# Turning the normalised tiles of one layer for the Strassen products: sums before the turning, or behind it

## The chip, the cores and the metric

One NeuronCore of a Trainium2 chip runs the whole layer as one program. The metric is device time in microseconds (us), the median of the runs shown. Engines are TensorE (PE in the profile; its weight loads are PEld), VectorE (DVE), ScalarE (ACT), GpSimd (POOL) and SyncE (SP, which issues the DMAs).

## The reference, cut to what matters

```python
h = h + jnp.concatenate([oA, oB], axis=-1) @ w_out     # output projection, 1024 tokens x 1024
hn = rms_norm(h, norm_ffn)
ab = hn @ w_ffn_in                                     # 1024 x (2 * 2816)
h = h + (gelu(causal_conv(ab[:, :2816]) + conv_b) * ab[:, 2816:]) @ w_ffn_out
```

Everything is float32. What is at stake is the stretch from the output projection to the first products of `hn @ w_ffn_in`.

## The kernel before, in words

Every float32 operand of a matmul is split in a high and a low part of type `fp32r`: ACT copies (that rounds, "hi"), VectorE subtracts the copy from the original ("lo"), and three matmuls take the place of one (hi hi, hi lo, lo hi). Each engine has its own program, written out in order by hand, with waits on semaphores; the order in which an engine's work stands is the order in which it runs.

**The projection.** `h` is 8 tiles of 128 tokens. They are projected in the order `O_TILE = (0, 4, 1, 5, 2, 6, 3, 7)`; below, tile i is the i-th of that order, and a pair j is tiles 2j and 2j+1, that is, a tile of the first 512 tokens and its partner in the second 512. Six rows of weights (`O_ROWS`) are left for this loop: `oproj(i, rows)` issues 6 matmuls of 128x512 for each row, so 36 for a tile, into PSUM banks 0 and 1 (even i) or 2 and 3 (odd i). Tiles 0 and 1 are begun earlier; the loop on TensorE runs over i = 2 to 7. For each tile VectorE adds the result to `h` (L1469, signals `h_mid`), ACT squares it (L796), VectorE makes the mean (L1194), GpSimd raises it to -0.5 (L687), and VectorE writes the normalised tile to `xs[:, i % 2]` (L1474, signals `xs1_ready`). SyncE stores each `h` tile to DRAM (L574), so that its place can take the token sums `hx`.

**The Strassen operands.** `hn @ w_ffn_in` is done by Winograd's form of Strassen's algorithm with 7 products. In it the token side needs, with B11, B21 (first tokens, first and second 512 features) and B12, B22 (second tokens), all with features on the partitions: B11, B21, B22 and the sums T1 = B12 - B11, T2 = B22 - T1, T3 = B22 - B12, T4 = B21 - T2. Features are put on the partitions by a transpose on TensorE: a matmul with the identity, 128x128 at a time. Before, the sums are made from the normalised tiles in SBUF: T1, T2, T4 on VectorE (L1410 through `minus`, in the loop behind the odd tile), T3 on GpSimd (L714), into the buffers `t_tmp`. Then TensorE turns them: `x_turn(g, j)` with g = 1: the even tile (8 transposes, L1729), g = 2: T1 and B22 (4 + 4), g = 3: T2 and T3 (4 + 4), g = 4: T4 (4; all of these L1968). The numbers `turn_no` give the order of the 16 groups, `turn_bank` alternates banks 4 and 5 with 6 and 7. Each group is split from PSUM, the high part by ACT's `x_hi(g, j)` (L793), the low part by VectorE's `x_lo(g, j)` (L1185). In the loop on odd i the groups of the pair before stand between rows of weights; the last pair's groups 2, 3 and 4 stand among the first products.

**The first products.** The 22 blocks f of 128 columns of `w_ffn_in` (a block holds one of the conv half and one of the gate half) give 7 products each: `p1` to `p7`, 12 matmuls of 128x512, each into a bank of its own (`bank_of`). `order` lists them: p1 and p2 of blocks 0 and 1, then p6, p7, p5, p4, p3 of block 0, of block 1, and then 7 of each further block. Their weight operands are split into a ring of 9 places by `op_hi(k)` and `op_lo(k)`; k is the position in `order`, so operands 0 to 3 are those of p1 and p2. Weight sums: s1 and s3 on GpSimd (L717, L714), s2 and s4 on VectorE (L1410). `p1_out` (ACT) copies product 1 out of its bank, and `c11(f)` (VectorE, L1499) adds product 2 to it; `p2(f)` for f >= 1 waits for `c11` of the block before, as they share bank 1. "Product 6" below is p6 of block 0.

```python
        def p2(f):
            if f >= 1:
                pe.wait_ge(S.c11, f)
            product(2, f, x_b21)
```

Of the kernel before, what the change touches and what calls it, by code (L numbers as in the profile page):

```python
# [63 lines left out]
def build(nc, x, p, w_in, w_out, sinks, lambda_q, lambda_k, subln_gain, rel_bias, norm_mix, norm_ffn,  # L64
# [140 lines left out]
    t_tmp = {1: conv[:, 0:HALF], 2: conv[:, HALF:D], 3: u3_buf, 4: a_buf[:, HALF + 4:D + 4]}  # L205
# [43 lines left out]
    def u_raw(s):  # L249
# [3 lines left out]
    turn_no = {(1, 0): 1, (2, 0): 2, (3, 0): 3, (1, 1): 4, (4, 0): 5, (2, 1): 6, (3, 1): 7, (1, 2): 8, (4, 1): 9,  # L253
               (2, 2): 10, (3, 2): 11, (1, 3): 12, (4, 2): 13, (2, 3): 14, (3, 3): 15, (4, 3): 16}

    def turn_bank(g, j):
        return 4 if turn_no[g, j] % 2 else 6
# [16 lines left out]
    t_tok t3_tok op_hi op_lo prod s1 s2 s3 s4 p1_out u2 u4 tap0 c11 c12 c21 c22 conv_done gelu_done  # L274
# [403 lines left out]
    def _(pool):  # L678
# [40 lines left out]
        def s1(f):  # L719
            w_there(pool, f, 1)  # L720
            if f == 0:
                pool.wait_ge(S.oproj, 1)
            if f == 1:
                pool.wait_ge(S.tr1, turn_no[2, 3])
                pool.wait_ge(S.t_tok, 4)
            if f >= 2:
                pool.wait_ge(S.op_lo, nth[5, f - 1] + 1)
            plus(s_tmp(1, f), w_half(f, 1, 0), w_half(f, 1, 1), S.s1)

        def s3(f):  # L730
            w_there(pool, f, 0)
            if f == 0:
                pool.wait_ge(S.tr1, turn_no[2, 3])
                pool.wait_ge(S.t_tok, 4)
                pool.wait_ge(S.t3_tok, 4)
            else:
                pool.wait_ge(S.op_lo, nth[7, f - 1] + 1)
            minus(s_tmp(3, f), w_half(f, 0, 0), w_half(f, 1, 0), S.s3)

        for i in range(NT):  # L740
            power(stat[:, i:i + 1], stat[:, 8 + i:9 + i], S.ms1, S.pow1, i)
            if i % 2 == 1:
                pool.wait_ge(S.xs1_ready, i + 1)
                if i >= 3:
                    pool.wait_ge(S.tr1, turn_no[3, i // 2 - 1])
                minus(t_tmp[3], xs[:, 1, HALF:D], xs[:, 1, 0:HALF], S.t3_tok)
            if i == 4:
                s1(0)
# [42 lines left out]
    def _(act):  # L791
# [221 lines left out]
        def x_hi(g, j):  # L1013
            act.wait_ge(S.tr1, turn_no[g, j])
            b = turn_bank(g, j)
            src = ps[:, b:b + 2, :]
            if g <= 2:
                t = j + 4 * (g - 1)
                copy(act_t[:, 0, :, t * P:(t + 1) * P], src.rearrange("p b (k n) -> p (b k) n", k=4), S.xhi1)
            elif g == 3:  # L1020
                act.wait_ge(x_again[j], 32)
                act.wait_ge(x_again[j + 4], 32)
                copy(hx[:, :, 0:HALF].rearrange("p (u j) n -> p u j n", u=2)[:, :, j, :], src, S.xhi1)
            else:
                copy(t4x[:, j, 0:HALF], ps[:, b, :], S.xhi1)

        for i in range(NT):
            j = i // 2
            if i == 2:
                x_hi(1, 0)  # L1030
            if i >= 3 and i % 2 == 1:
                x_hi(2, j - 1)
                x_hi(3, j - 1)
                if i == NT - 1:
                    op_hi(2)
                    op_hi(3)
                x_hi(1, j)
                x_hi(4, j - 1)
            act.wait_ge(S.h_mid, i + 1)
            if i >= 2:  # L1040
                act.wait_ge(S.tr1, turn_no[1 + i % 2, j - 1])
                act.wait_ge(S.t_tok, j)
                act.wait_ge(S.t3_tok, j)
# [29 lines left out]
        op_hi(4)  # L1073
        x_hi(2, 3)
        x_hi(3, 3)
# [99 lines left out]
    def _(dve):  # L1175
# [241 lines left out]
        def s4(f):  # L1417
            if f == 0:
                dve.wait_ge(S.tr1, turn_no[2, 3])
                dve.wait_ge(S.t3_tok, 4)  # L1420
            dve.wait_ge(S.s2, f + 1)
            minus(s_tmp(4, f), w_half(f, 0, 1), s_tmp(2, f)).then_inc(S.s4, 1)
# [18 lines left out]
        def x_lo(g, j):  # L1441
            dve.wait_ge(S.xhi1, turn_no[g, j])
            b = turn_bank(g, j)
            src = ps[:, b:b + 2, :]
            if g <= 2:
                sl = slice((j + 4 * (g - 1)) * P, (j + 4 * (g - 1) + 1) * P)
                low(act_t[:, 1, :, sl], src.rearrange("p b (k n) -> p (b k) n", k=4), act_t[:, 0, :, sl], S.xlo1)
            elif g == 3:
                dst = hx[:, :, :].rearrange("p (u j) n -> p u j n", u=2)[:, :, j, :]
                low(dst[:, :, HALF:D], src, dst[:, :, 0:HALF], S.xlo1)  # L1450
            else:
                low(t4x[:, j, HALF:D], ps[:, b, :], t4x[:, j, 0:HALF], S.xlo1)
# [3 lines left out]
        for i in range(NT):  # L1456
            t, j, b = O_TILE[i], i // 2, 2 * (i % 2)
            if i == 2:
                x_lo(1, 0)
            if i >= 3 and i % 2 == 1:  # L1460
                x_lo(2, j - 1)
                x_lo(3, j - 1)
                if i == NT - 1:
                    op_lo(2)
                    op_lo(3)
                x_lo(1, j)
                x_lo(4, j - 1)
# [253 lines left out]
    def _(pe):  # L1721
# [244 lines left out]
        def turn4(src, bank):  # L1966
            for k in range(4):
                ins = nc.tensor.transpose(ps[:, bank, k * P:(k + 1) * P], src[:, k * P:(k + 1) * P], ident[:, :])  # L1968
            return ins

        def x_turn(g, j):
            n, b = turn_no[g, j], turn_bank(g, j)
            if n >= 3:
                pe.wait_ge(S.xlo1, n - 2)
            if g == 1:
                pe.wait_ge(S.xs1_ready, 2 * j + 1)
                turn8(xs[:, 0, :], b, S.tr1)
            elif g == 2:
                pe.wait_ge(S.t_tok, j + 1)
                turn4(t_tmp[1], b)  # L1980
                turn4(xs[:, 1, HALF:D], b + 1).then_inc(S.tr1, 1)
            elif g == 3:
                pe.wait_ge(S.t3_tok, j + 1)
                turn4(t_tmp[2], b)
                turn4(t_tmp[3], b + 1).then_inc(S.tr1, 1)
            else:
                turn4(t_tmp[4], b).then_inc(S.tr1, 1)

        for i in range(2, NT):
# [3 lines left out]
            if i == 2:  # L1993
                oproj(i, O_ROWS[1:3])
                x_turn(1, 0)
                oproj(i, O_ROWS[3:])
            elif i % 2 == 1:
                x_turn(2, j - 1)
                oproj(i, O_ROWS[1:2])
                x_turn(3, j - 1)  # L2000
                oproj(i, O_ROWS[2:4])
                x_turn(1, j)
                oproj(i, O_ROWS[4:5])
                x_turn(4, j - 1)
# [203 lines left out]
```

## Time and profile before

| | us |
|---|---|
| median of 3 runs | 1230.97 |
| lowest and highest run | 1227.92, 1232.18 |
| span of the profiled execution | 1229.7 |
| TensorE busy in it | 1197.1 (97%) |
| VectorE, ScalarE, GpSimd busy | 867.3 (71%), 517.8 (42%), 250.2 (20%) |

The span runs from the first to the last instruction of the profiled execution; of that execution's own time no other figure is given than this span. A busy share is an average over stages. Which wait ends last in a stage is read from the chain of waits and from the timelines, where each line gives start, duration, engine, code line, output and inputs, how many instructions are merged in it, and in brackets how long the engine was idle before it and which instruction ended that. The duration of a merged TensorE line reaches to the modelled end of its last matmul, which overlaps the next line; lengths of stretches on TensorE are therefore taken from start to start.

### The profile page before, as it was taken

Reading aid. Unit: us, or ns where it says so; the run is one execution under the profiler, and the core shown is the slowest. Engines: PE = TensorE matmul, PEld = TensorE weight load, DVE = VectorE, ACT = ScalarE, POOL = GpSimd, SP = SyncE. Lnnn points to the kernel's source line nnn. Section 1 sums busy time; section 2 is a strip of 40 time slices with the busy share of each in tenths; the row PEclk is TensorE's granted clock in tenths of the full one; section 3 lists DMA queues with packets and bytes.
Section 4 is the critical chain, followed back from the end, with each engine's and each line's share of the span. In section 5 each row is a group of like instructions: output and inputs, shape, how many; then the busy total and the mean of one; then the engine's idle time right before and its main releaser. Section 6 shows DMA issues by size and latency. Waiting matters only on the chain.

```text
span 1229.7 us, 17128 instructions
## 1 busy us (share of the span) xinstructions
PE 1197.1 (97%) x6167; PEld 1001.8 (81%) x6167; DVE 867.3 (71%) x1514; ACT 517.8 (42%) x1045; POOL 250.2 (20%) x291
## 2 busy tenths in 40 slices
PE   8999999999888999999999999999999999999997
PEld 7998887788676888888888888888888888888886
DVE  5433786877886577877787777877777999964443
ACT  4312665565655224433343343343344444733321
POOL 0000000344455122232332323323210000000000
PEclk9999999999899999999999999999999999999999
DMA  7464233111831512242322333233499533620101
GB/s 217 89 90 91 50 89 76 42 40 69 222 139 42 164 52 81 82 128 94 121 87 89 125 103 112 95 94 112 146 345 312 172 95 103 225 75 26 43 35 51
DMA packets 127916, 136.08 MB, mean 111 GB/s; under 512 B 15714, under 2 KB 93274, under 8 KB 127770
## 3 DMA queue, kind: packets, MB, share of 16 engines
q1 hardware_dynamic: 127834, 135.00, 36.1%
q8 instruction: 49, 0.80, 0.3%
q14 instruction: 33, 0.27, 0.1%
HBM read 96.77 MB, written 37.22 MB: 109 GB/s over the span
## 4 chain that ended last, share of the span: by engine, by line
PE 61%; issue 4%; DVE 2%; POOL 1%; ACT 1%; POOLq 0%; DVEq 0%; ACTq 0%
PE ps L1723 60%; PE ps L1729 1%; DVE xs L1474 1%; DVE h L1469 0%; DVE conv L1410 0%; POOL stat L687 0%; ACT xs L796 0%; DVE act_t L1185 0%; POOL stat L706 0%; POOL bias_a L712 0%; POOL more_f L714 0%; PE ps L2118 0%; ACT wbuf L793 0%; POOL o_t L709 0%; DVE h L1688 0%
## 5 line engine op out<-in xcount | busy, mean ns | idle before, releaser
L1723 PE MATMUL ps<-act_t,wbuf 128*128 128x512 f32 x1200 | 280.1, 389 | 0.5 <-DVE a_buf L1499 0.5
L1723 PEld LDWEIGHTS ps<-act_t,wbuf 128*128 128x128 f32 x1200 | 225.2, 188 | 47.5 <-DVE a_buf L1499 0.8
L1723 PE MATMUL ps<-wbuf 128*128 128x512 f32 x912 | 214.8, 390 | 0.0
L1723 PEld LDWEIGHTS ps<-wbuf 128*128 128x128 f32 x912 | 170.6, 188 | 35.1
L1723 PE MATMUL ps<-act_t,wq 128*128 128x512 f32 x624 | 152.2, 396 | 3.6 <-DVE wq L1187 3.0
L1723 PEld LDWEIGHTS ps<-act_t,wq 128*128 128x128 f32 x624 | 114.3, 188 | 30.8 <-issue 7.5
L687 POOL TENSOR_TENSOR stat<-stat 128x1 f32<-128x1 f32 x32 | 17.6, 549 | 420.9 <-DVE stat L1194 420.9
L793 ACT ACTIVATE wbuf<-raw 128x512 fp32r<-128x512 f32 (+1 forms) x107 | 69.0, 646 | 73.9 <-PE ps L1723 63.8
L1723 PE MATMUL ps<-hx,wbuf 128*128 128x512 f32 x408 | 95.7, 389 | 0.0
L1185 DVE TENSOR_TENSOR wbuf<-raw,wbuf 128x512 fp32r<-128x512 f32 (+1 forms) x107 | 87.4, 818 | 11.5 <-ACT wbuf L793 11.2
L1723 PEld LDWEIGHTS ps<-hx,wbuf 128*128 128x128 f32 x408 | 76.5, 188 | 15.9
L875 ACT ACTIVATE e_t<-ps,small 128x128 f32<-128x128 f32 (+7 forms) x64 | 47.3, 740 | 63.4 <-DVE small L1314 62.3
L793 ACT ACTIVATE wbuf<-xs 128x512 fp32r<-128x512 f32 x66 | 39.8, 624 | 71.9 <-DVE xs L1410 54.2
L1723 PE MATMUL ps<-wbuf,act_t 128*128 128x512 f32 x288 | 69.6, 395 | 0.0
L1723 PEld LDWEIGHTS ps<-wbuf,act_t 128*128 128x128 f32 x288 | 52.9, 188 | 10.5
L1723 PE MATMUL ps<-wq,act_t 128*128 128x384 f32 (+1 forms) x384 | 59.5, 315 | 1.5 <-DVE wq L1185 1.5
L1723 PEld LDWEIGHTS ps<-wq,act_t 128*128 128x128 f32 x384 | 57.9, 193 | 2.0 <-issue 1.7
L1723 PE MATMUL ps<-act_t,more 128*128 128x512 f32 x240 | 56.8, 389 | 0.0
L714 POOL TENSOR_TENSOR wbuf_f<-wbuf_f 128x512 f32<-128x512 f32 x33 | 52.2, 1581 | 18.6 <-DVE wbuf_f L1553 15.6
L1185 DVE TENSOR_TENSOR a_t<-ps,a_t 128x512 fp32r<-128x512 f32 (+4 forms) x64 | 44.6, 715 | 15.4 <-ACT a_t L793 15.3
L1723 PEld LDWEIGHTS ps<-act_t,more 128*128 128x128 f32 x240 | 45.0, 188 | 9.4
L1185 DVE TENSOR_TENSOR wbuf<-xs,wbuf 128x512 fp32r<-128x512 f32 x66 | 50.3, 762 | 0.5
(208 smaller groups left out, 1962.8 us busy)
## 6 DMA issues: line engine op xcount, KB each, us to landing
u_ops<-wbuf_f SPq DMA_DIRECT2D x77, 256.0 KB, 2.2
raw<-u_ops SPq DMA_DIRECT2D x77, 256.0 KB, 2.7
raw<-in_w_ffn_in SPq DMA_DIRECT2D x33, 512.0 KB, 3.8
g_ffn<-in_w_ffn_in SPq DMA_DIRECT2D x11, 512.0 KB, 3.9
act_f<-in_w_ffn_out SPq DMA_DIRECT2D x21, 256.0 KB, 4.3
w_raw<-in_w_in SPq DMA_DIRECT2D x10, 512.0 KB, 4.4
wbuf_f<-in_w_ffn_out SPq DMA_DIRECT2D x18, 256.0 KB, 5.9
x_in<-in_x SPq DMA_DIRECT2D x8, 512.0 KB, 3.8
```

Of the source, the lines that this page charges most:

```text
L687: nc.gpsimd.tensor_tensor(dst, src, stat[:, 63:64], ALU.pow).then_inc(done, 1)
L714: nc.gpsimd.tensor_tensor(dst, a, b, ALU.subtract).then_inc(done, 1)
L793: nc.scalar.activation(dst, src, ACT.Copy, scale=scale).then_inc(done, 1)
L875: nc.scalar.activation(e_t[:, pr, m, 0:w], psf[:, at:at + w], ACT.Exp, scale=-1.0, bias=small[:, o + 2 + m:o + 3 + m], accum_out=small[:, ...
L1185: ins = nc.vector.tensor_tensor(dst, src, hi.bitcast(F32), ALU.subtract)
L1474: nc.vector.scalar_tensor_tensor(out=xs[:, i % 2, :], in0=h[:, t, :], scalar=stat[:, 8 + i:9 + i], in1=g_ffn[:, :], op0=ALU.mult, op1=ALU. ...
L1723: return nc.tensor.matmul(dst, lhs, rhs, start=start, stop=stop)
L1729: ins = nc.tensor.transpose(psf[:, bank * HALF + k * P:bank * HALF + (k + 1) * P], src[:, k * P:(k + 1) * P], ident[:, :])
```

## The change

Only plain tiles are turned, one group of 8 transposes for each tile: `x_turn(1, j)` the even tile into banks 4 and 5 (B11, B21), `x_turn(2, j)` the odd tile into banks 6 and 7 (B12, B22). In the loop over i the turning of tile i-1 stands behind the fourth row of weights; in i = 2 both tiles of pair 0 are turned. The last tile is turned behind p2(0). Then ACT copies B12 to SBUF (`x_b12`), VectorE makes T3 = B22 - B12, T1, T2 and T4 from PSUM and the copy, and the splits of T1 to T4 read SBUF. B22 alone is a fifth split, g = 5. `split_no` numbers the splits. GpSimd's T3 is gone. On VectorE `x_sum3` stands ahead of the even tile's h add, T1, T2, the low split of B22 and T4 (`x_sums`) between that add and the mean, and three low splits behind the normalised tile. Behind the loop the order on VectorE, ACT and TensorE changes too.

```diff
-    t_tmp = {1: conv[:, 0:HALF], 2: conv[:, HALF:D], 3: u3_buf, 4: a_buf[:, HALF + 4:D + 4]}
+    t_tmp = {1: u3_buf, 2: conv[:, 0:HALF], 3: conv[:, HALF:D], 4: a_buf[:, HALF + 4:D + 4]}
...
+    def turn_no(g, j):
+        return 2 * j + g
+
+    def split_no(g, j):
+        order = [(1, 0)] + [o for j in range(4) for o in ((5, j), (3, j), (2, j), (4, j), (1, j + 1)) if o != (1, 4)]
+        return order.index((g, j)) + 1
...
             power(stat[:, i:i + 1], stat[:, 8 + i:9 + i], S.ms1, S.pow1, i)
-            if i % 2 == 1:
-                pool.wait_ge(S.xs1_ready, i + 1)
-                if i >= 3:
-                    pool.wait_ge(S.tr1, turn_no[3, i // 2 - 1])
-                minus(t_tmp[3], xs[:, 1, HALF:D], xs[:, 1, 0:HALF], S.t3_tok)
             if i == 4:
                 s1(0)
...
+        def x_b12(j):
+            act.wait_ge(S.tr1, turn_no(2, j))
+            copy(t_tmp[1], ps[:, 6, :], S.b12_out)
 
         for i in range(NT):
             j = i // 2
             if i == 2:
                 x_hi(1, 0)
+            if i >= 2 and i % 2 == 0:
+                x_b12(j - 1)
+                x_hi(5, j - 1)
+            if i == NT - 1:
+                op_hi(2)
+                op_hi(3)
             if i >= 3 and i % 2 == 1:
-                x_hi(2, j - 1)
-                x_hi(3, j - 1)
-                if i == NT - 1:
-                    op_hi(2)
-                    op_hi(3)
                 x_hi(1, j)
-                x_hi(4, j - 1)
...
             square(h[:, O_TILE[i], :], xs[:, i % 2, :], stat[:, 56 + i % 2:57 + i % 2], S.sq1)
+            if i >= 2 and i % 2 == 0:
+                x_hi(3, j - 1)
+                x_hi(2, j - 1)
+                x_hi(4, j - 1)
...
         p1_out(0)
         op_hi(4)
+        x_b12(3)
+        x_hi(5, 3)
+        x_hi(3, 3)
         x_hi(2, 3)
-        x_hi(3, 3)
         op_hi(5)
         x_hi(4, 3)
         op_hi(6)
...
+        b11, b21, b22 = ps[:, 4, :], ps[:, 5, :], ps[:, 7, :]
+
+        def x_sum3(j):
+            dve.wait_ge(S.b12_out, j + 1)
+            dve.wait_ge(S.xhi1, split_no(5, j))
+            minus(t_tmp[3], b22, t_tmp[1]).then_inc(S.t3_made, 1)
+
+        def x_sums(j):
+            dve.wait_ge(S.t3_made, j + 1)
+            minus(t_tmp[1], t_tmp[1], b11).then_inc(S.t_made, 1)
+            dve.wait_ge(S.t_made, 3 * j + 1)
+            minus(t_tmp[2], b22, t_tmp[1]).then_inc(S.t_made, 1)
+            x_lo(5, j)
+            dve.wait_ge(S.t_made, 3 * j + 2)
+            minus(t_tmp[4], b21, t_tmp[2]).then_inc(S.t_made, 1)
...
             if i == 2:
                 x_lo(1, 0)
+            if i >= 2 and i % 2 == 0:
+                x_sum3(j - 1)
+            if i == NT - 1:
+                op_lo(2)
+                op_lo(3)
             if i >= 3 and i % 2 == 1:
-                x_lo(2, j - 1)
-                x_lo(3, j - 1)
-                if i == NT - 1:
-                    op_lo(2)
-                    op_lo(3)
                 x_lo(1, j)
-                x_lo(4, j - 1)
             dve.wait_ge(S.oproj, i + 1)
             nc.vector.tensor_tensor(h[:, t, :], ps[:, b:b + 2, :].rearrange("p b n -> p (b n)"), h[:, t, :],
                                     ALU.add).then_inc(S.h_mid, 1)
+            if i >= 2 and i % 2 == 0:
+                x_sums(j - 1)
             dve.wait_ge(S.sq1, i + 1)
             mean_eps(stat[:, 56 + i % 2:57 + i % 2], stat[:, i:i + 1], D, S.ms1)
...
-            if i % 2 == 1:
...
-                link(minus(t_tmp[1], xs[:, 1, 0:HALF], xs[:, 0, 0:HALF]))
-                link(minus(t_tmp[2], xs[:, 1, HALF:D], t_tmp[1]))
...
-                minus(t_tmp[4], xs[:, 0, HALF:D], t_tmp[2]).then_inc(S.t_tok, 1)
+            if i >= 2 and i % 2 == 0:
+                x_lo(3, j - 1)
+                x_lo(2, j - 1)
+                x_lo(4, j - 1)
             if i in (4, 6):
                 op_lo(i // 2 - 2)
...
         op_lo(4)
-        c11(0)
+        x_sum3(3)
+        x_sums(3)
+        x_lo(3, 3)
         x_lo(2, 3)
-        x_lo(3, 3)
         op_lo(5)
         x_lo(4, 3)
+        c11(0)
         op_lo(6)
...
         def x_turn(g, j):
+            pe.wait_ge(S.xs1_ready, 2 * j + g)
+            if j >= 1:
+                pe.wait_ge(S.t_made, 3 * j)
+                if g == 1:
+                    pe.wait_ge(S.xlo1, split_no(1, j - 1))
+                else:
+                    pe.wait_ge(S.xlo1, split_no(5, j - 1))
+            turn8(xs[:, g - 1, :], 2 + 2 * g, S.tr1)
...
             if i == 2:
                 oproj(i, O_ROWS[1:3])
                 x_turn(1, 0)
-                oproj(i, O_ROWS[3:])
...
+                oproj(i, O_ROWS[3:5])
+                x_turn(2, 0)
                 oproj(i, O_ROWS[5:])
             else:
-                oproj(i, O_ROWS[1:])
+                oproj(i, O_ROWS[1:4])
+                x_turn(1 + (i + 1) % 2, (i - 1) // 2)
+                oproj(i, O_ROWS[4:])
...
         pe.wait_ge(S.h_mid, NT - 1)
-        pe.wait_ge(S.xlo1, turn_no[1, 3])
+        pe.wait_ge(S.xlo1, split_no(1, 3))
         p1(0)
         p2(0)
+        x_turn(2, 3)
         p1(1)
-        x_turn(2, 3)
-        x_turn(3, 3)
         p2(1)
-        x_turn(4, 3)
         pe.wait_ge(S.h_mid, NT)
-        pe.wait_ge(S.xlo1, turn_no[3, 3])
+        pe.wait_ge(S.xlo1, split_no(3, 3))
         p6(0)
-        pe.wait_ge(S.xlo1, turn_no[4, 3])
         for f in range(2):
             if f == 1:
                 p6(1)
             p7(f)
+            if f == 0:
+                pe.wait_ge(S.xlo1, split_no(2, 3))
             p5(f)
+            if f == 0:
+                pe.wait_ge(S.xlo1, split_no(4, 3))
             p4(f)
             p3(f)
```

## Rows read from the trace of the kernel before

**Rows 1.** The page: busy time of the engines; a group of DMA issues (us to landing last).

```profile
PE 1197.1 (97%) x6167; PEld 1001.8 (81%) x6167; DVE 867.3 (71%) x1514; ACT 517.8 (42%) x1045; POOL 250.2 (20%) x291
...
raw<-in_w_ffn_in SPq DMA_DIRECT2D x33, 512.0 KB, 3.8
```

**Rows 2.** The chain that ended last: start, us, what, up to the gate stage.

```profile
486.64 598.44 PE ps L1723 x2640
```

**Rows 3.** Timeline of TensorE in the projection: start, us, what, idle before.

```profile
416.73 1.03 PE L1729 MATMUL ps<-ident,xs 128*128 128x128 f32 x8
...
442.74 0.60 PE L1968 MATMUL ps<-ident,conv 128*128 128x128 f32 x4
...
448.92 1.09 PE L1729 MATMUL ps<-ident,xs 128*128 128x128 f32 x8
449.77 1.64 PE L1723 MATMUL ps<-wbuf,act_t 128*128 128x512 f32 x6
451.25 0.60 PE L1968 MATMUL ps<-ident,a_buf 128*128 128x128 f32 x4
```

**Rows 4.** The same timeline, first products: product 1, the fourth product, product 6.

```profile
472.57 5.61 PE L1723 MATMUL ps<-act_t,more 128*128 128x512 f32 x24
...
483.17 3.03 PE L1723 MATMUL ps<-act_t,wbuf 128*128 128x512 f32 x12 [0.53 <-DVE a_buf L1499]
...
486.40 3.91 PE L1723 MATMUL ps<-hx,wbuf 128*128 128x512 f32 x16
```

**Rows 5.** Timeline of VectorE: sums, h add, mean, tile; c11 and splits.

```profile
419.17 0.69 DVE L1410 TENSOR_TENSOR conv<-xs 128x512 f32<-128x512 f32 x1
419.90 1.67 DVE L1410 TENSOR_TENSOR conv<-xs,conv 128x512 f32<-128x512 f32 x1
...
441.58 1.23 DVE L1469 TENSOR_TENSOR h<-ps,h 128x1024 f32<-128x1024 f32 x1 [0.47 <-PE ps L1723]
444.02 0.15 DVE L1194 TENSOR_SCALAR stat<-stat 128x1 f32<-128x1 f32 x1 [1.22 <-ACT xs L796]
444.83 2.30 DVE L1474 SCALAR_TENSOR_TENSOR xs<-h,stat,g_ffn 128x1024 f32<-128x1024 f32 x1 [0.66 <-POOL stat L687]
...
476.03 1.29 DVE L1474 SCALAR_TENSOR_TENSOR xs<-h,stat,g_ffn 128x1024 f32<-128x1024 f32 x1 [0.67 <-POOL stat L687]
...
482.44 0.68 DVE L1499 TENSOR_TENSOR a_buf<-ps,wbuf_f 128x512 f32<-128x512 f32 x1
483.04 1.21 DVE L1185 TENSOR_TENSOR act_t<-ps,act_t 128x1024 fp32r<-128x1024 f32 x1
484.17 1.21 DVE L1185 TENSOR_TENSOR hx<-ps,hx 128x1024 fp32r<-128x1024 f32 x1
```

**Rows 6.** Timeline of ACT: high splits from PSUM, of 512 and 1024 columns.

```profile
432.03 0.60 ACT L793 ACTIVATE wbuf<-ps 128x512 fp32r<-128x512 f32 x1 [0.81 <-PE ps L1968]
...
450.05 1.03 ACT L793 ACTIVATE act_t<-ps 128x1024 fp32r<-128x1024 f32 x1 [2.96 <-PE ps L1729]
```

**Rows 7.** Timeline of GpSimd: T3 of pair 0, and s1 of block 0.

```profile
419.22 1.80 POOL L714 TENSOR_TENSOR more_f<-xs 128x512 f32<-128x512 f32 x1 [1.40 <-DVE xs L1474]
...
444.77 1.28 POOL L717 TENSOR_TENSOR gel<-raw 128x512 f32<-128x512 f32 x1
```

**Rows 8.** Windows of TensorE: stretch, its length, busy (instructions), granted clock, DMA share, GB/s.

```profile
26.00:30.00 4.00, 3.96 (x18) 0.57 0.41 131
319.00:327.00 8.00, 5.97 (x32) 0.57 1.03 259
388.00:392.00 4.00, 4.00 (x19) 0.57 0.00 0
402.00:1085.00 683.00, 682.35 (x3065) 1.00 0.40 132
```

**Rows 9.** Timeline of TensorE in the attention stage: two idle times ahead of falls.

```profile
317.78 0.30 PE L1898 MATMUL ps<-ident,bias_a 128*128 128x128 f32 x1 [1.61 <-POOL bias_a L712]
...
387.04 1.06 PE L1915 MATMUL ps<-ident,e_t 128*128 128x128 f32 x8 [2.07 <-DVE act_t L1185]
```

More of the change, by code:

```diff
@@ L252, in build @@
     O_TILE = (0, 4, 1, 5, 2, 6, 3, 7)
[L253 to L257, printed above, removed]
+    def turn_no(g, j):
[3 more added lines that the diff above has]
+        return order.index((g, j)) + 1
     ut = wbuf[:, 10 * D:14 * D].rearrange("p (s l n) -> p s l n", s=2, l=2)
@@ L273, in build @@
     wo_hi wo_lo mix_c mix_45 mix_23 c_done c_added oproj h_mid sq1 ms1 pow1 xs1_ready tr1 xhi1 xlo1 gffn_in o_row
-    t_tok t3_tok op_hi op_lo prod s1 s2 s3 s4 p1_out u2 u4 tap0 c11 c12 c21 c22 conv_done gelu_done
+    b12_out t3_made t_made op_hi op_lo prod s1 s2 s3 s4 p1_out u2 u4 tap0 c11 c12 c21 c22 conv_done gelu_done
     u_ready su u_st pad_zero t_low h_fin wp_in wg_hi wg_lo gple_in gfin_in sq2 ms2 pow2 xs2_ready tr2 xhi2 xlo2 gate_done pp_done
@@ L723, in s1 @@
             if f == 1:
-                pool.wait_ge(S.tr1, turn_no[2, 3])
-                pool.wait_ge(S.t_tok, 4)
+                pool.wait_ge(S.tr1, turn_no(2, 3))
             if f >= 2:
@@ L732, in s3 @@
             if f == 0:
-                pool.wait_ge(S.tr1, turn_no[2, 3])
-                pool.wait_ge(S.t_tok, 4)
-                pool.wait_ge(S.t3_tok, 4)
+                pool.wait_ge(S.tr1, turn_no(2, 3))
             else:
@@ L1013, in x_hi @@
         def x_hi(g, j):
[L1014 to L1019, printed above, removed]
+            if g == 1:
+                act.wait_ge(S.tr1, turn_no(1, j))
+            elif g == 5:
+                act.wait_ge(S.tr1, turn_no(2, j))
+            else:
+                act.wait_ge(S.t_made, 3 * j + {2: 1, 3: 2, 4: 3}[g])
+            if g == 1:
+                copy(act_t[:, 0, :, j * P:(j + 1) * P], ps[:, 4:6, :].rearrange("p b (k n) -> p (b k) n", k=4), S.xhi1)
+            elif g == 2:
+                copy(act_t[:, 0, 0:4, (j + 4) * P:(j + 5) * P], t_tmp[1].rearrange("p (k n) -> p k n", k=4), S.xhi1)
+            elif g == 5:
+                copy(act_t[:, 0, 4:8, (j + 4) * P:(j + 5) * P], ps[:, 7, :].rearrange("p (k n) -> p k n", k=4), S.xhi1)
             elif g == 3:
@@ L1022, in x_hi @@
                 act.wait_ge(x_again[j + 4], 32)
-                copy(hx[:, :, 0:HALF].rearrange("p (u j) n -> p u j n", u=2)[:, :, j, :], src, S.xhi1)
-            else:
-                copy(t4x[:, j, 0:HALF], ps[:, b, :], S.xhi1)
+                copy(hx[:, :, 0:HALF].rearrange("p (u j) n -> p u j n", u=2)[:, :, j, :],
+                     conv[:, :].rearrange("p (u n) -> p u n", u=2), S.xhi1)
+            else:
+                copy(t4x[:, j, 0:HALF], t_tmp[4], S.xhi1)
+        def x_b12(j):
+            act.wait_ge(S.tr1, turn_no(2, j))
+            copy(t_tmp[1], ps[:, 6, :], S.b12_out)
         for i in range(NT):
@@ L1030, in _ @@
                 x_hi(1, 0)
-            if i >= 3 and i % 2 == 1:
-                x_hi(2, j - 1)
-                x_hi(3, j - 1)
-                if i == NT - 1:
-                    op_hi(2)
-                    op_hi(3)
+            if i >= 2 and i % 2 == 0:
[4 more added lines that the diff above has]
+                op_hi(3)
+            if i >= 3 and i % 2 == 1:
                 x_hi(1, j)
-                x_hi(4, j - 1)
             act.wait_ge(S.h_mid, i + 1)
             if i >= 2:
-                act.wait_ge(S.tr1, turn_no[1 + i % 2, j - 1])
-                act.wait_ge(S.t_tok, j)
-                act.wait_ge(S.t3_tok, j)
+                act.wait_ge(S.tr1, turn_no(1 + i % 2, j - 1))
             square(h[:, O_TILE[i], :], xs[:, i % 2, :], stat[:, 56 + i % 2:57 + i % 2], S.sq1)
+            if i >= 2 and i % 2 == 0:
+                x_hi(3, j - 1)
+                x_hi(2, j - 1)
+                x_hi(4, j - 1)
             if i in (4, 6):
@@ L1418, in s4 @@
             if f == 0:
-                dve.wait_ge(S.tr1, turn_no[2, 3])
-                dve.wait_ge(S.t3_tok, 4)
+                dve.wait_ge(S.tr1, turn_no(2, 3))
             dve.wait_ge(S.s2, f + 1)
@@ L1441, in x_lo @@
         def x_lo(g, j):
[L1442 to L1447, printed above, removed]
+            dve.wait_ge(S.xhi1, split_no(g, j))
+            sl = slice((j if g == 1 else j + 4) * P, (j + 1 if g == 1 else j + 5) * P)
+            if g == 1:
+                low(act_t[:, 1, :, sl], ps[:, 4:6, :].rearrange("p b (k n) -> p (b k) n", k=4), act_t[:, 0, :, sl], S.xlo1)
+            elif g == 2:
+                low(act_t[:, 1, 0:4, sl], t_tmp[1].rearrange("p (k n) -> p k n", k=4), act_t[:, 0, 0:4, sl], S.xlo1)
+            elif g == 5:
+                low(act_t[:, 1, 4:8, sl], ps[:, 7, :].rearrange("p (k n) -> p k n", k=4), act_t[:, 0, 4:8, sl], S.xlo1)
             elif g == 3:
                 dst = hx[:, :, :].rearrange("p (u j) n -> p u j n", u=2)[:, :, j, :]
-                low(dst[:, :, HALF:D], src, dst[:, :, 0:HALF], S.xlo1)
+                low(dst[:, :, HALF:D], conv[:, :].rearrange("p (u n) -> p u n", u=2), dst[:, :, 0:HALF], S.xlo1)
             else:
-                low(t4x[:, j, HALF:D], ps[:, b, :], t4x[:, j, 0:HALF], S.xlo1)
+                low(t4x[:, j, HALF:D], t_tmp[4], t4x[:, j, 0:HALF], S.xlo1)
+        b11, b21, b22 = ps[:, 4, :], ps[:, 5, :], ps[:, 7, :]
[11 more added lines that the diff above has]
+            minus(t_tmp[4], b21, t_tmp[2]).then_inc(S.t_made, 1)
         dve.wait_ge(S.gffn_in, 16)
@@ L1475, in _ @@
                                            in1=g_ffn[:, :], op0=ALU.mult, op1=ALU.mult).then_inc(S.xs1_ready, 1)
-            if i % 2 == 1:
-                dve.wait_ge(S.xs1_ready, i + 1)
-                if j >= 1:
-                    dve.wait_ge(S.tr1, turn_no[3, j - 1])
-                link(minus(t_tmp[1], xs[:, 1, 0:HALF], xs[:, 0, 0:HALF]))
-                link(minus(t_tmp[2], xs[:, 1, HALF:D], t_tmp[1]))
-                if j >= 1:
-                    dve.wait_ge(S.tr1, turn_no[4, j - 1])
-                minus(t_tmp[4], xs[:, 0, HALF:D], t_tmp[2]).then_inc(S.t_tok, 1)
+            if i >= 2 and i % 2 == 0:
+                x_lo(3, j - 1)
+                x_lo(2, j - 1)
+                x_lo(4, j - 1)
             if i in (4, 6):
@@ L1964, in _ @@
         oproj(1, O_ROWS[4:])
[L1966 to L1969, printed above, removed]
         def x_turn(g, j):
[L1972 to L1987, printed above, removed]
+            pe.wait_ge(S.xs1_ready, 2 * j + g)
+            if j >= 1:
+                pe.wait_ge(S.t_made, 3 * j)
+                if g == 1:
+                    pe.wait_ge(S.xlo1, split_no(1, j - 1))
+                else:
+                    pe.wait_ge(S.xlo1, split_no(5, j - 1))
+            turn8(xs[:, g - 1, :], 2 + 2 * g, S.tr1)
         for i in range(2, NT):
@@ L1995, in _ @@
                 x_turn(1, 0)
-                oproj(i, O_ROWS[3:])
[L1997 to L2004, printed above, removed]
+                oproj(i, O_ROWS[3:5])
+                x_turn(2, 0)
                 oproj(i, O_ROWS[5:])
             else:
-                oproj(i, O_ROWS[1:])
+                oproj(i, O_ROWS[1:4])
+                x_turn(1 + (i + 1) % 2, (i - 1) // 2)
+                oproj(i, O_ROWS[4:])
         x_b11 = [[act_t[:, b, k, 0:HALF] for k in range(4)] for b in range(2)]
```

## The prediction

> **What bounds the kernel now.** I read the page first, then the chain of waits, then TensorE's timeline from the projection to the first products, and last the timelines of the engines that feed it. On the page TensorE is busy for 97% of the span [rows 1]; the chain ends its preparation with one unbroken run of 2640 matmuls from 486.64 us on, 598.44 us long [rows 2]. That gives the two facts on which the sum rests: a 128x512 matmul costs 598.44/2640 = 0.2267 us, and whatever moves the start of that run (product 6 of block 0, first matmul at 486.40 [rows 4]) moves the end of the kernel by as much, since nothing inside the run waits. From the first turning at 416.73 [rows 3] to 486.40 are 69.67 us. They hold 246 matmuls (18 left of tile 2, 36 in each of five tiles, 12 in each of four products), 55.77 us. The other 13.90 us are 112 transposes and TensorE's waits, of which 0.53 us before the fourth product is the longest [rows 4].
>
> **What goes away.** A pair of tiles takes 28 transposes before (8, 8, 8, 4) and 16 after (8, 8); the four pairs fall from 112 to 64. A run of eight costs 449.77 - 448.92 = 0.85 us to the next matmul's start, and the six matmuls behind it take 1.48 to the next transpose instead of 6 x 0.2267 = 1.36 [rows 3], so 0.97 us in all. Eight such runs are 7.76 us against 13.90 now: TensorE's own need falls by 6.1 us. GpSimd's difference (1.80 us, four times) goes too; it lies beside other work and counts nothing, but the VectorE sum that ran beside it took 1.67 us where the one before took 0.69 [rows 5, 7].
>
> **What comes in.** The sums move from ahead of the turning to behind it, so that they now stand in VectorE's order between what TensorE waits for. Three waits follow; between them TensorE has fixed cover.
>
> *Wait 1, in the loop (three times).* An even tile's h add starts 0.20 us after its matmuls end (441.58 against 442.74 - 1.36 = 441.38 [rows 3, 5]). Behind it VectorE now does T1, T2, the split of b22 and T4 before it may give out the mean. None of these was seen with just these operands; the nearest rows are an add of PSUM with SBUF, 0.68 us, and SBUF alone, 0.69 [rows 5], so I take 0.69 with a pitch of 0.60, and 0.73 where an instruction waits for the one before (419.17 to 419.90 [rows 5]). Even a free sum would only take the whole wait away; at the 1.67 us of the slowed one, three would add about 3 us to it: these are its ends. From the h add: 1.14 (a 1024-wide pitch, 483.04 to 484.17) + 0.73 + 0.60 + 0.60 + 0.60 + 0.81 (mean to normalised tile, 444.02 to 444.83) + 1.29 (the tile, 476.03) = 5.77 [rows 5]. So the tile is there 0.20 + 5.77 + 0.10 for a hand-off = 6.07 us after TensorE ended that projection. TensorE turns it after four rows of the next tile, 24 matmuls: 5.44 + 0.1 us. It waits 0.5 us. In the first pair only six matmuls follow the second turning, and the h add waits for the copy and the sum T3 in front of it, 0.4 more; in the second GpSimd's sum for block 0 (1.28 us) runs beside the tile, which took 2.30 us instead of 1.29 in the same place [rows 5, 7], 1.0 more. 0.9 + 1.5 + 0.5 = **2.9 us**. The odd tiles have no sums behind their add: 0.20 + 1.14 + ACT's square and the rest come to some 4.8 us, inside the 5.44.
>
> *Wait 2, ahead of product 1.* After tile 6's normalised form VectorE does three splits of pair 2, three splits of weights (operands 1, 2, 3), and the split of tile 6's turned form, for which product 1 waits: 1.14 + 5 x 0.60 + 1.22 = 5.4 us. TensorE covers 0.97 + 12 x 0.2267 = 3.7, and 0.1 for the hand-off: **1.6 us**.
>
> *Wait 3, ahead of the fourth product.* The second product of block 1 needs block 0's sum c11, which frees its PSUM bank. VectorE did it at 482.44, before any split [rows 5], and TensorE resumed behind it at once [rows 4]. The change puts it behind the whole last pair. With X the start of the last turning: ACT's copy of b12 starts at X + 1.13 (448.92 to 450.05 [rows 3, 6]), two copies of 0.60 [rows 6] reach X + 2.4 with hand-offs; T3, T1 and T2 0.73 each, b22's split 0.60, T4 0.60, the 1024-wide split 1.14, then T1's split, block 0's s4, operand 5 and T4's split at 0.60 each, c11 itself 0.69: X + 9.9. TensorE has 0.97 + 2.72 = 3.7 us of work. It stands for **6.2 us**. The ACT copies in between end before VectorE needs them. The bounds are 0 (c11 does not hold the product; the order in the code excludes it) and 8 us, if GpSimd's sums beside it doubled two or three splits that now read SBUF.
>
> The sum at product 6 is 416.73 + 55.77 + 7.76 + 2.9 + 1.6 + 6.2 = 490.96, **4.6 us later** than 486.40.
>
> On the price of the sums the Trainium skill speaks against the change: VectorE: DVE Perf Modes, section on the TRN2 errata, gives VectorE's fixed part as 58 cycles from SBUF and 120 from PSUM, at 0.96 GHz an estimated 0.065 us more for each sum. Three sums on each of three loop paths and four at the end would make the total some 0.85 us worse. The rows (0.68 with PSUM, 0.69 without [rows 5]) show no such difference, and I take them.
>
> *The clock.* From 402 to 1085 us the granted clock is 1.00 now, 2.4 GHz [rows 8]. Behind an idle 2.07 us at 387.04 it fell to half, 1.2 GHz [rows 8, 9]: the mean over 388 to 392 is 0.57, a loss of 4 x 0.43 = 1.7 us. The same 1.7 us shows at 26 to 30; from 319 to 327, where several idle times followed each other (1.61 us the first [rows 9]), it is 3.4. Six idle microseconds should cost one such fall, **1.7 us**, with 0 (the low stretch lies within the wait itself) and 3.4 as ends.
>
> Elsewhere I cost nothing. SyncE's load of block 2's first weights waits for s4 and leaves perhaps 1 us later; it lands in about 3.8 us [rows 1], and its first user is ten products (27 us) behind product 6. GpSimd's own first sums wait for the last turning and still lie ahead of their splits. The extra ACT copies fill ACT's idle time. After product 6 VectorE is further ahead of TensorE than before, so nothing there waits.
>
> Total: 4.6 + 1.7 = **6.3 us slower**. The profiled execution spans 1229.7 us, which would become 1236.0; it lies 1.3 under the median of the runs, 1230.97, on which I put the prediction: **1237.3 us**.
>
> **Rivals.** (a) *Only the transposes count*: VectorE's chain behind the last turning fits under TensorE's cover (3.7 us instead of 9.9) and the loop has no wait; then the time is 1230.97 - 6.1 = 1224.9. For it: ACT and VectorE had idle time in this stretch, and the sums no longer run against GpSimd. Against it: the order in the code. It decides where all waits together stay under 2.4 us. Chance 0.08. (b) *The waits nearly pay for the transposes*: the clock stays up and the loop waits vanish, since tiles come earlier than I reckon: 4.6 - 2.9 = 1.7, 1232.7. For it: those waits are differences of half a microsecond. Chance 0.13. (c) *The clock falls in the loop too*: the waits of 1.5 us ahead of tile 4's turning and of product 1 each halve it, once 1.7, twice 3.4 more: 1239.0 to 1240.7. For it: 1.61 us followed by another wait did it at 320. Against: an idle 1.6 alone is less than the 2.07 that did. Chance 0.14. The Trainium skill (TensorE: Matmul & The Clock Gate, section on PSUM-queue depth-cycling) tells of a kernel whose clock swings because of frequent short idles between groups; the fall at 320 us agrees in kind.
>
> **How the numbers follow.** The forecast has 0.65, with its own range from 4 (no fall of the clock) to 9 us (a second fall, or slowed splits). A measurement here tells 0.3%, 3.7 us, from no change. Forecast and (c) together hold 0.79; some 0.03 of the forecast's low end lies within 3.7 us. So slower 0.76, same 0.16, faster 0.08. The range leaves out (a) and the worst of (c): from 1232.0, which takes in (b) with little to spare, to 1242.0.
>
> **What would show it.** In the changed trace: 64 transposes in eight runs of eight between 416 and about 485 us; TensorE idle ahead of the turnings of tiles 2, 4 and 6 by about half to one and a half microseconds, put down to the normalised tile; about 1.6 ahead of product 1 put down to a split; and one of about 6 us ahead of the fourth product put down to the c11 add, with the granted clock near 0.5 behind it. Product 6 then starts near 491 to 493. The prediction is wrong if that last wait is under 3 us, or if the run of 2640 matmuls is no longer unbroken.

## The result and the profile after

The changed kernel took 1235.31 us in the median of 4 runs (1234.49 to 1235.51) against 1230.53 before (4 runs): a ratio of 1.0044, with a 95% interval of 1.003 to 1.0058. It is 4.8 us slower; forecast were 6.3.

TensorE's timeline in the profile after, from the first turning to product 6 (start, us, what, count, and in brackets the idle time before it and what ended it), answers to [rows 3, 4]:

```profile
413.79 1.03 PE L1752 MATMUL ps<-ident,xs 128*128 128x128 f32 x8
...
426.08 1.09 PE L1752 MATMUL ps<-ident,xs 128*128 128x128 f32 x8 [0.81 <-DVE xs L1500]
...
445.83 1.09 PE L1752 MATMUL ps<-ident,xs 128*128 128x128 f32 x8 [1.41 <-DVE xs L1500]
...
464.57 1.09 PE L1752 MATMUL ps<-ident,xs 128*128 128x128 f32 x8 [0.40 <-DVE xs L1500]
...
469.90 5.69 PE L1746 MATMUL ps<-act_t,more 128*128 128x512 f32 x24 [1.48 <-issue]
475.43 1.04 PE L1752 MATMUL ps<-ident,xs 128*128 128x128 f32 x8
476.22 2.97 PE L1746 MATMUL ps<-act_t,wbuf 128*128 128x512 f32 x12
485.25 5.32 PE L1746 MATMUL ps<-act_t,wbuf 128*128 128x512 f32 x12 [6.05 <-DVE a_buf L1520]
490.40 5.61 PE L1746 MATMUL ps<-hx,wbuf 128*128 128x512 f32 x24
```

Each of the 64 transposes is where the change puts it, and TensorE now waits five times where it waited 0.53 us once [rows 4]. Ahead of product 1 the view names "issue", which is time for which it found no releaser; VectorE's timeline below names it. The fourth product stands in one line of 5.32 us where the same 12 matmuls took 3.03 before [rows 4].

VectorE in the same profile: tile 2's h add and what stands behind it, the split for which product 1 waits (468.58), and the last pair up to c11 (L1520); it answers to [rows 5].

```profile
420.29 1.22 DVE L1493 TENSOR_TENSOR h<-ps,h 128x1024 f32<-128x1024 f32 x1
421.42 0.68 DVE L1418 TENSOR_TENSOR more_f<-more_f,ps 128x512 f32<-128x512 f32 x1
422.13 0.69 DVE L1418 TENSOR_TENSOR conv<-ps,more_f 128x512 f32<-128x512 f32 x1
422.74 0.68 DVE L1193 TENSOR_TENSOR act_t<-ps,act_t 128x512 fp32r<-128x512 f32 x1
423.34 0.68 DVE L1418 TENSOR_TENSOR a_buf<-ps,conv 128x512 f32<-128x512 f32 x1
423.94 0.14 DVE L1202 TENSOR_SCALAR stat<-stat 128x1 f32<-128x1 f32 x1
424.74 1.29 DVE L1500 SCALAR_TENSOR_TENSOR xs<-h,stat,g_ffn 128x1024 f32<-128x1024 f32 x1 [0.66 <-POOL stat L688]
...
443.49 2.29 DVE L1500 SCALAR_TENSOR_TENSOR xs<-h,stat,g_ffn 128x1024 f32<-128x1024 f32 x1 [0.66 <-POOL stat L688]
...
468.58 1.22 DVE L1193 TENSOR_TENSOR act_t<-ps,act_t 128x1024 fp32r<-128x1024 f32 x1
...
477.69 0.69 DVE L1418 TENSOR_TENSOR conv<-ps,more_f 128x512 f32<-128x512 f32 x1 [1.39 <-ACT act_t L786]
...
484.51 0.68 DVE L1520 TENSOR_TENSOR a_buf<-ps,wbuf_f 128x512 f32<-128x512 f32 x1
```

From the h add (420.29) to the mean (423.94) are 3.65 us, all of it sums and one split; the mean before came 2.44 us after its h add, and waited for ACT's square in that time [rows 5]. From T3 at 477.69 to c11's end at 485.19 VectorE has no gap. The split at 468.58 ends at 469.80, product 1 starts at 469.90.

The windows of TensorE ahead of the last pair and about the long wait (stretch, its length, busy and count, granted clock, DMA share, GB/s):

```profile
402.00:474.00 72.00, 67.89 (x325) 1.00 0.24 87
...
474.00:483.00 9.00, 5.20 (x27) 1.00 0.21 60
483.00:485.00 2.00, 0.00 (x0) 0.60 0.15 40
485.00:490.00 5.00, 4.75 (x11) 0.50 0.64 189
490.00:500.00 10.00, 10.00 (x45) 0.99 0.38 107
```

The clock fell to half within the wait and stayed there for almost the whole fourth product; the 0.99 behind 490 leaves some 0.2 us of it. In the chain that ended last, the matmuls from the fourth product on (its 12 and the 2640 behind it) form one piece, so what delays product 6 delays the end:

```profile
485.25 603.74 PE ps L1746 x2652
```

**Two numbers for one change.** The profiled execution took 1235.51 us with a span of 1233.6. From the first turning to product 6 it needs 490.40 - 413.79 = 76.61 us, against 69.67 before: 6.9 us more. Behind product 6 both profiles need the same (743.3 us before, 743.2 after), and so do the six profiles of the experiments (743.2 or 743.3). The spans differ only by 3.9 us because the profile before reached its first turning 2.94 us later (416.73 against 413.79), in a part whose work the change does not touch. Most of that arose near 25 us. TensorE's timelines there, before first, then after:

```profile
25.23 1.09 PE L1729 MATMUL ps<-ident,xs 128*128 128x128 f32 x8 [1.84 <-DVE xs L1220]
...
34.98 1.04 PE L1729 MATMUL ps<-ident,xs 128*128 128x128 f32 x8
```

```profile
23.98 1.09 PE L1752 MATMUL ps<-ident,xs 128*128 128x128 f32 x8 [0.63 <-DVE xs L1228]
...
32.26 1.03 PE L1752 MATMUL ps<-ident,xs 128*128 128x128 f32 x8
```

Before, the wait was 1.2 us longer, and the same work behind it took 9.75 us instead of 8.28, at a mean granted clock of 0.86 from 20 to 32 us against 1.00. By 387 us before was only 1.85 us behind (387.04 [rows 9] against 385.19); then its clock fell once more (0.84 from 384 to 395 us against 1.00), which cost 1.25 us (6.34 us to the next turning that waits, at 393.38, against 5.09 to 390.28). The first turning lies between 412.74 and 418.86 in the eight profiles of this study. So the stretch from the first turning to product 6 is the sharper measure of an edit, and the runs below are read by it as well as by their times.

### The profile page after: what moved, and what is told of

Read it like the earlier page. It is cut to its first block, busy times and chain, and to the rows that moved or that the text cites. A ratio compares the mean times of both kernels' runs of the same rounds, so it can differ in the third digit from the quotient of the medians.

```text
span 1233.6 us, 17029 instructions
## 1 busy us (share of the span) xinstructions
PE 1191.7 (97%) x6119; PEld 995.3 (81%) x6119; DVE 866.6 (70%) x1522; ACT 521.8 (42%) x1053; POOL 242.5 (20%) x287
## 4 chain that ended last, share of the span: by engine, by line
PE 63%; issue 2%; DVE 2%; POOL 1%; ACT 0%; DVEq 0%; POOLq 0%; ACTq 0%
PE ps L1746 62%; PE ps L1752 1%; DVE xs L1500 0%; DVE h L1493 0%; DVE conv L1418 0%; POOL stat L688 0%; DVE act_t L1193 0%; POOL stat L707 0%; POOL bias_a L713 0%; DVE more_f L1418 0%; DVE a_buf L1418 0%; PE ps L2124 0%; POOL o_t L710 0%; DVE h L1711 0%; DVE conv L1708 0%
```

## The experiments

All are built on the changed kernel unless it is said otherwise, and each ratio is to the kernel before on the same chip.

**c11 back in its place** (c11_first)**.** My theory was that c11's place causes the long wait, and the wait the fall of the clock.

```diff
         op_lo(4)
+        c11(0)
         x_sum3(3)
         x_sums(3)
...
         x_lo(4, 3)
-        c11(0)
```

> The changed kernel with one line moved: c11 of block 0 stands again right behind operand 4's split, ahead of T3. Theory (c11's place causes the 6.05 us wait, and that wait the fall of the clock): the wait before the fourth product goes; product 6 then waits some 0.4 us for the split of T2 and T3, which ends at 482.2 as now, and starts near 482.3 instead of 490.4; the granted clock stays 1.00. From the first turning to product 6 about 68.5 us instead of 76.6; time near 1227.2, 3 us below the kernel before. Rival (the last pair's sums and splits behind the turning are what is late, and another wait takes c11's place): product 6 still starts at 487 or later and the time stays above 1232.

Measured: 1229.12 us (11 runs), ratio 0.9997 (0.9987 to 1.0006). TensorE's timeline, from the first turning through product 1 and the fourth product to product 6:

```profile
414.45 1.03 PE L1752 MATMUL ps<-ident,xs 128*128 128x128 f32 x8
...
470.56 5.73 PE L1746 MATMUL ps<-act_t,more 128*128 128x512 f32 x24 [1.48 <-issue]
...
476.91 5.70 PE L1746 MATMUL ps<-act_t,wbuf 128*128 128x512 f32 x24
482.98 5.72 PE L1746 MATMUL ps<-hx,wbuf 128*128 128x512 f32 x24 [0.36 <-issue]
```

Products three and four run in one piece, product 6 waits 0.36 us, and the stretch is 482.98 - 414.45 = 68.53 us, to a tenth what was expected. One instruction's place was worth 8.1 us. The rival is out. My forecast of the time was wrong: I set 8.1 us against the time after, whose early part was shorter than that of before; by the stretch the gain on the kernel before is 1.1 us, and the times do not tell that from nothing.

**A warm wait.** Does the fall of the clock cost what it seems to, and is it the idleness that causes it?

```diff
         p1(1)
+        pe.wait_ge(S.h_mid, NT)
+        for _ in range(48):
+            nc.tensor.transpose(ps[:, 2, 0:P], ident[:, :], ident[:, :])
         p2(1)
-        pe.wait_ge(S.h_mid, NT)
```

> The changed kernel with 48 transposes of the identity, 48 x 0.109 = 5.2 us, put on TensorE ahead of the fourth product, into the bank that product 6 overwrites: the wait for c11 stays, but TensorE is not idle in it. Theory (the clock fell because of that idle time): c11 ends near 485.2 as now, the clock stays 1.00, the fourth product takes 2.7 us instead of 5.15, product 6 starts near 488.0, and the time falls by 2.4 us to about 1232.9. Rival (the clock falls for what happened earlier, or the low stretch costs nothing since VectorE is the limit there): product 6 starts at 490.4 and the time stays at 1235.3.

Measured: 1236.05 us, ratio 1.0043 (1.0027 to 1.006). The timeline from the first turning, and the windows of the wait:

```profile
418.86 1.03 PE L1752 MATMUL ps<-ident,xs 128*128 128x128 f32 x8
...
484.12 5.40 PE L2077 MATMUL ps<-ident 128*128 128x128 f32 x48
490.32 3.02 PE L1746 MATMUL ps<-act_t,wbuf 128*128 128x512 f32 x12 [0.80 <-DVE a_buf L1520]
493.18 5.60 PE L1746 MATMUL ps<-hx,wbuf 128*128 128x512 f32 x24
```

```profile
484.00:490.00 6.00, 5.53 (x50) 1.00 0.03 8
490.00:493.00 3.00, 2.68 (x12) 1.00 0.54 159
```

The clock stays up and the fourth product takes 2.86 us to product 6, so it was the idleness that made the clock fall. The stretch is 74.32 us, 2.3 less than after. So the wait itself costs 5.8 us (74.32 - 68.53, with c11 early), and the fall behind it 2.3 to 2.4 more. The time does not show this; my forecast of 1232.9 us was missed by 3.2. In the profiled execution, the longest of the four (1238.3 us), the first turning came at 418.86, 5.1 us later than in the profile after; the other three have no trace.

**The cost alone, in the kernel before.** Only c11 of block 0 is moved, four instructions back.

```diff
         op_lo(4)
-        c11(0)
         x_lo(2, 3)
         x_lo(3, 3)
         op_lo(5)
+        c11(0)
         x_lo(4, 3)
```

> The kernel before, with only c11 of block 0 moved: behind operand 5's split instead of ahead of the last pair's splits. Everything else of the change is left out. Theory: four instructions now stand ahead of c11, 1.13 + 1.13 + 0.60 + 0.60 = 3.5 us, so TensorE's wait before the fourth product grows from 0.53 to about 4.0 us; the clock falls behind it as it did behind 2.07 us, for 0 to 2.4 us more; time 1234.0 to 1236.4. Rival (c11's place matters only together with the sums from PSUM): no change, 1230.5.

Measured: 1235.25 us, ratio 1.0051 (1.0033 to 1.007). The timeline, first turning, fourth product and product 6, and the windows behind the wait:

```profile
418.14 1.03 PE L1729 MATMUL ps<-ident,xs 128*128 128x128 f32 x8
...
488.48 5.49 PE L1723 MATMUL ps<-act_t,wbuf 128*128 128x512 f32 x12 [4.43 <-DVE a_buf L1499]
...
494.46 5.72 PE L1723 MATMUL ps<-hx,wbuf 128*128 128x512 f32 x24
```

```profile
488.00:494.00 6.00, 5.52 (x14) 0.50 0.30 87
```

The wait grew by 3.9 us, and the clock fell as it does after. The stretch of 76.32 us is nearly that of the whole change (76.61): this one line makes the kernel before as slow as the change does, without a sum from PSUM.

**All even tiles turned later.** This tests whether the waits in the loop can be covered.

```diff
-                oproj(i, O_ROWS[1:4])
+                cut = 5 if i % 2 else 4
+                oproj(i, O_ROWS[1:cut])
                 x_turn(1 + (i + 1) % 2, (i - 1) // 2)
-                oproj(i, O_ROWS[4:])
+                oproj(i, O_ROWS[cut:])
```

> The changed kernel with the even tile's turning one row of weights later in the odd tiles' projections (30 matmuls ahead of it instead of 24, 1.36 us more cover). Theory (waits 1 are the sums between the h add and the mean, 6.1 us against 5.5 of cover): the waits of 0.81 and 1.41 ahead of these turnings go, the 0.40 too, but that one is given back ahead of product 1, which hangs on VectorE; the odd tile's h add comes up to 0.9 us later and its turning waits some 0.15; sum -1.9 us, first turning to product 6 about 74.7, time near 1233.4. Rival (VectorE is the limit through the whole loop): the waits only move to the odd tiles' turnings, and the stretch stays above 76.

Measured: 1234.53 us, ratio 1.0045 (1.0027 to 1.0062). A miss: the stretch is 489.58 - 412.74 = 76.84 us, not 74.7. The timeline of tiles 2 and 5 (their turnings) and of product 1, and the window of product 1:

```profile
412.74 1.03 PE L1752 MATMUL ps<-ident,xs 128*128 128x128 f32 x8
...
425.43 1.04 PE L1752 MATMUL ps<-ident,xs 128*128 128x128 f32 x8
...
452.53 1.09 PE L1752 MATMUL ps<-ident,xs 128*128 128x128 f32 x8 [0.60 <-DVE xs L1500]
...
467.54 7.33 PE L1746 MATMUL ps<-act_t,more 128*128 128x512 f32 x24 [2.12 <-issue]
```

```profile
467.50:473.00 5.50, 5.46 (x17) 0.69 0.24 96
```

The three waits are gone as expected, and 0.60 came ahead of tile 5's turning, as VectorE's work on tile 4 (its form took 2.31 us here) now delays tile 5's h add. But 2.12 us now stand ahead of product 1, and behind them the clock fell in this execution: 5.5 x 0.31 = 1.7 us went with it. The gain of some 1.4 us on the waits was more than given back. That the stretch lies above 76, as the rival said, is due to the clock; the waits did shrink, and without the fall it would be an estimated 76.84 - 1.7 = 75.1.

**Two moves, with c11 in its place** (c11_and_moves)**.** GpSimd's s1 goes to where VectorE is idle, and two weight splits from ahead of the split that product 1 needs to behind the last h add.

```diff
+            if i == 4:
+                pool.wait_ge(S.xs1_ready, 4)
+                s1(0)
             power(stat[:, i:i + 1], stat[:, 8 + i:9 + i], S.ms1, S.pow1, i)
-            if i == 4:
-                s1(0)
...
-            if i == NT - 1:
-                op_lo(2)
-                op_lo(3)
             if i >= 3 and i % 2 == 1:
                 x_lo(1, j)
...
                                      ALU.add).then_inc(S.h_mid, 1)
+            if i == NT - 1:
+                op_lo(2)
+                op_lo(3)
```

> c11_first with two more moves. GpSimd makes s1 of block 0 behind the third pair's odd tile instead of beside tile 4's normalised form (it waits for xs1_ready 4 and stands ahead of the power of tile 4); VectorE splits operands 2 and 3 behind the h add of the last tile instead of ahead of the split that product 1 waits for. Theory (these two own 1.0 us of the 1.42 us wait and 1.2 us of the 1.48): tile 4's normalised form takes 1.29 us instead of 2.29 and TensorE waits 0.4 for it; product 1 waits 0.3; nothing is given back later, as VectorE stood idle 1.2 us behind that h add. First turning to product 6 about 66.3 us against 68.53 in c11_first and 69.67 before; time 3.4 us below the kernel before, some 1226.1. Rival (the last tile's chain is the limit, so the end only waits longer ahead of product 6 or the last turning): stretch at 68 or more.

Measured: 1226.55 us (12 runs), ratio 0.9974 (0.9963 to 0.9985). TensorE at the first turning, at tile 4's, product 1 and product 6; then VectorE's line of tile 4's normalised form:

```profile
414.32 1.04 PE L1753 MATMUL ps<-ident,xs 128*128 128x128 f32 x8
...
445.37 1.09 PE L1753 MATMUL ps<-ident,xs 128*128 128x128 f32 x8 [0.41 <-DVE xs L1501]
...
468.23 5.73 PE L1747 MATMUL ps<-act_t,more 128*128 128x512 f32 x24 [0.28 <-issue]
...
480.66 5.73 PE L1747 MATMUL ps<-hx,wbuf 128*128 128x512 f32 x24 [0.37 <-issue]
```

```profile
444.03 1.29 DVE L1501 SCALAR_TENSOR_TENSOR xs<-h,stat,g_ffn 128x1024 f32<-128x1024 f32 x1 [0.66 <-POOL stat L688]
```

and GpSimd's sum, first in the profile after, beside that form, then here, where VectorE stands idle:

```profile
443.42 1.28 POOL L718 TENSOR_TENSOR gel<-raw 128x512 f32<-128x512 f32 x1
...
435.13 1.29 POOL L718 TENSOR_TENSOR gel<-raw 128x512 f32<-128x512 f32 x1 [1.40 <-DVE xs L1501]
```

The stretch is 66.34 us. Both waits shrank by what was claimed for them, and nothing was given back. The tile's form took 1.29 us once GpSimd's sum no longer ran beside it, 2.29 with it; the sum took 1.28 and 1.29 us. Here only VectorE was held up. The Trainium skill (GPSIMD Engine Reference, section Specifications) lists GpSimd's access to SBUF as shared with VectorE, with contention for VectorE instructions that have two SBUF inputs; this run agrees, with 1.0 us.

**And tile 2's turning later, alone.** The same cut as above, only for i = 3.

```diff
+                cut = 5 if i == 3 else 4
```

> c11_and_moves with tile 2's turning one row of weights later (30 matmuls ahead of it in tile 3's projection instead of 24), for this turning alone. Theory: the wait of 0.81 us goes, and nothing comes in its place, as in the run with all turnings later the odd tile behind it did not wait; stretch about 65.5 us; time some 1225.3, 4.2 us below the kernel before. Rival (VectorE passes the delay on to tile 3's turning): no gain over c11_and_moves, 66.3 us.

Measured: 1225.61 us (12 runs), ratio 0.9966 (0.9955 to 0.9977). TensorE at the first turning, at tile 2's and at product 6:

```profile
415.57 1.03 PE L1753 MATMUL ps<-ident,xs 128*128 128x128 f32 x8
...
428.25 1.04 PE L1753 MATMUL ps<-ident,xs 128*128 128x128 f32 x8
...
481.11 5.72 PE L1747 MATMUL ps<-hx,wbuf 128*128 128x512 f32 x24 [0.36 <-issue]
```

The wait ahead of tile 2's turning is gone, tile 3's does not wait either, and the stretch is 65.54 us: 4.1 below before, 11.1 below after. The 0.8 us less than in the run before this one is read from the stretch; the intervals of the two ratios overlap. By its ratio this version beats both kernels. Without the four waits that are left (0.40, 0.40, 0.27, 0.36) it would need 64.1 us; by the prediction's prices TensorE's need is 55.77 + 7.76 = 63.5.

## Why the prediction was right

*What goes away*: right, but somewhat less. With c11 back in its place, where the long wait is gone, 68.53 us are 63.53 of matmuls and runs of eight, 4.5 of waits that the timeline names (0.81, 1.42, 0.40, 1.48, 0.36) and 0.5 that it puts to no wait. Without the named waits these are 64.06 us, against 69.67 - 0.53 = 69.14 before: TensorE's need fell by 5.1 us, not by 6.1. The 13.90 us of the prediction contain the wait of 0.53 before the fourth product, and its 7.76 lack the 0.5 without a name. The waits take most of the gain back.

*Wait 1*: 0.9, 1.5 and 0.5 us were forecast, 0.81, 1.41 and 0.40 came, each put down to the normalised tile, as forecast. That 1.0 us of the second is GpSimd's sum is shown by the run that moved it.

*Wait 2*: 1.6 forecast, 1.48 measured; the run with two splits moved left 0.28.

*Wait 3*: 6.2 forecast, 6.05 measured, put down to c11. From the last turning (475.43) to c11's end (485.19) are 9.8 us, 9.9 by the prediction (whose terms as listed add up to 10.0). That c11's place decides whether there is a wait is shown from both sides: with c11 early it is gone, and with c11 late the kernel before waits 4.43 us instead of 0.53. How long it is depends on what stands ahead of c11; behind the late sums it is 6.05 us.

*The clock*: the right mechanism, mis-sized. I took 1.7 us from the falls behind short waits; it cost 2.3 to 2.4 (76.61 - 74.32 between after and the warm wait; 5.15 - 2.72 on the fourth product). All of the dense work up to about 490.2 ran at half. This lies inside the ends that I gave, 0 and 3.4. The row that I read it from does not repeat, though: behind the wait of 2.07 us [rows 9] the clock fell before, and behind the same wait, 2.06 us, in the profile after it stayed at 1.00 (the table at the end).

*The sum* up to product 6 was 4.6 + 1.7 = 6.3 us; measured are 4.5 + 2.4 = 6.9. That the 4.6 fits to a tenth is partly luck: the waits came to 10.15 us instead of 10.7, and the 0.5 without a name made up for it. Product 6 itself started at 490.40, just ahead of the 491 to 493 that I gave, only because the first turning came early. That the median moved only by 4.8 I did not foresee. In the profiled pair the difference lies in the part ahead of the first turning; that it does so in the other runs is not shown, as they have no trace. The interval of the ratio, 3.7 to 7.1 us, holds 6.3 and 6.9.

*Prices*: the sums from PSUM took 0.68 to 0.69 us, also where a sum on GpSimd ran beside them (VectorE from 478.42, GpSimd from 478.13 to 479.42), while the sum from SBUF had taken 1.67 in such company [rows 5, 7]. The 0.065 us more that the prediction estimated from the Trainium skill (VectorE: DVE Perf Modes, section on the TRN2 errata) did not show.

*Rivals*: (a) did not happen; with c11 in its place 4.5 us of waits remain, and only the last run comes near to it, with 1.4 us of waits. (b) fell with the measured loop waits and the fall of the clock. (c) did not happen after: 1.41 and 1.48 us idle left the clock at 1.00 (402 to 474 us). In the run with all turnings later it did once, behind 2.12 us ahead of product 1.

## What to carry to other kernels

Where work moves from ahead of a step to behind it, write down for each engine the order in which its instructions now stand, and look in it for those that some other engine waits for: an instruction that was ready early and now stands behind late ones takes on their lateness. Here that one line cost more than all 48 transposes saved, and putting it back, with one sum on GpSimd and two weight splits moved as well, turned a loss into a gain. Where the start of a program varies between executions, measure an edit by a stretch with fixed ends.

## What the runs showed that I had not expected

The same wait came with and without a fall of the clock. Ahead of product 1, idle 1.48 us left the granted clock at 1.00, and idle 2.12 us, in one profile, was followed by half the clock and 1.7 us of lost work. Ahead of the fourth product, idle 4.43, 6.01 and 6.05 us were each followed by a fall; the last cost 2.4. One might take the length of a wait for what decides. But in the attention stage all eight profiles have a wait of 2.05 to 2.08 us ahead of the same eight transposes (387.04 in [rows 9]); behind it the clock fell in five of them and stayed at 1.00 in three. What decides at this length is not shown, so the fall behind 2.12 us need not come in each execution either. In the table are the start of the first turning, that wait, and the mean granted clock in three stretches ahead of the first turning.

| profile | first turning | wait | 20 to 32 us | 310 to 330 us | 384 to 395 us |
|---|---|---|---|---|---|
| all even tiles turned later | 412.74 | 2.06 | 1.00 | 0.91 | 1.00 |
| after | 413.79 | 2.06 | 1.00 | 0.83 | 1.00 |
| two moves, with c11 in its place | 414.32 | 2.05 | 1.00 | 0.83 | 0.84 |
| c11 back in its place | 414.45 | 2.08 | 1.00 | 0.83 | 1.00 |
| tile 2's turning later as well | 415.57 | 2.08 | 1.00 | 0.83 | 0.84 |
| before | 416.73 | 2.07 | 0.86 | 0.83 | 0.84 |
| before, c11 late | 418.14 | 2.07 | 0.86 | 0.83 | 0.84 |
| a warm wait | 418.86 | 2.07 | 0.72 | 0.83 | 0.84 |

And the kernels share the part ahead of the first turning, yet it ended between 412.74 and 418.86 us. The more falls of the clock a profile has there, the later it tends to be. The falls are not all of it: between before and after, a wait at 25 us that was 1.2 us longer counts as well.
